# First two token groups of a projection stage: K in order of arrival, V weights loaded later, another way to sum squares, and half of a norm's scaling on ScalarE

## The reference, cut to what matters

```python
def rmsnorm(x, g):
    xf = x.astype(jnp.float32)
    y = xf * lax.rsqrt(jnp.mean(xf * xf, axis=-1, keepdims=True) + RMS_EPS)
    return (y * g.astype(jnp.float32)).astype(x.dtype)

h = rmsnorm(x, norm_g)              # (S, 2048)
z = h @ w_in                        # columns q | k | v | f | g_A | u | v_B | g_B
k = z[..., OFF_K:OFF_V]             # 8 heads x 128, an output and input of the attention
v = z[..., OFF_V:OFF_F]
logf = log_sigmoid(z[..., OFF_F:OFF_GA] + b_f)
...                                 # attention with forget bias, gated MLP over 128-chunks
y = rmsnorm(x + concat(out_a, out_b) @ w_out, final_g)
```

## Time and profile before

| | us |
|---|---|
| three timed runs, median (lowest, highest) | 1661.77 (1661.71, 1662.76) |
| the profiled execution | 1658.95 |
| its span on the slowest core, core 4 (role 0) | 1655.4 |
| spans of role 0: cores 0, 2, 4, 6 | 1654.0, 1653.5, 1655.4, 1650.1 |
| spans of role 1: cores 1, 3, 5, 7 | 1645.0, 1646.6, 1633.8, 1640.2 |
| PE busy on core 4, share of the span | 1493.5, 90% |
| ACT, DVE, POOL busy on core 4 | 589.6, 548.0, 187.8 |

### The profile page before, as it was taken

One profiled execution on the slowest core, in us unless ns is written; L12 is line 12 of the kernel. 1 busy time (PEld: TensorE's weight loads), 2 busy tenths in 40 slices (PEclk: granted clock), 3 DMA queues, 4 the chain that ended last, 5 costly groups with the idle time before them and its releaser, 6 DMA issues.

```text
span 1655.4 us, 29925 instructions; the slowest of 8 cores (1633.8 to 1655.4 us)
## 1 busy us (share of the span) xinstructions
PE 1493.5 (90%) x10986; PEld 884.7 (53%) x11164; DVE 548.0 (33%) x1035; ACT 589.6 (36%) x1011; POOL 187.8 (11%) x328
## 2 busy tenths in 40 slices
PE   2688895999699999999999999999999989999996
PEld 1567762444244444444466775776766744444443
DVE  5478710000244433333442222222222222333333
ACT  2234310111455411111115666666666681111111
POOL 2111220111233200000001101101101110000000
PEclk9899997999799999999999999999999999999999
DMA  9956399886500131222231313313212065545543
GB/s 234 231 186 228 90 163 129 130 111 92 93 1 1 24 64 42 54 42 42 58 87 26 88 28 81 78 42 82 59 46 59 26 164 166 206 152 205 201 154 118
DMA packets 90982, 168.96 MB, mean 102 GB/s; under 512 B 27728, under 2 KB 69840, under 8 KB 82000
## 3 DMA queue, kind: packets, MB, share of 16 engines
q1 hardware_dynamic: 81472, 129.17, 28.5%
q0 software_dynamic: 9360, 37.79, 13.7%
HBM read 141.68 MB, written 63.04 MB: 124 GB/s over the span
## 4 chain that ended last, share of the span: by engine, by line
PE 75%; DMA 8%; DVE 8%; ACT 5%; issue 4%; POOL 1%; SPq 0%; ACTq 0%; DVEq 0%; POOLq 0%
PE psb L291 74%; ACT arena L1026 3%; DVE arena L403 3%; DMA kT<-arena 3%; DVE arena L380 3%; DMA vo<-arena 2%; DMA arena<-bs 1%; DVE arena L901 1%; DMA arena<-xT 1%; PE psb L1097 0%; DVE arena L1099 0%; POOL arena L383 0%; POOL arena L1029 0%; ACT arena L478 0%; DVE arena L1083 0%
## 5 line engine op out<-in xcount | busy, mean ns | idle before, releaser
L291 PE MATMUL psb<-arena 128*128 128x512 bf16 (+5 forms) x10826 | 1488.0, 296 | 146.8 <-POOL arena L383 34.4
L291 PEld LDWEIGHTS psb<-arena 128*128 128x128 bf16 (+1 forms) x11004 | 876.3, 98 | 753.2 <-issue 166.0
L1026 ACT ACTIVATE arena<-psb,arena 128x512 bf16<-128x512 f32 x480 | 301.0, 634 | 167.6 <-PE psb L291 160.2
L1184 ACT ACTIVATE arena<-arena 128x2048 bf16<-128x2048 f32 x20 | 38.2, 1910 | 237.9 <-DVE arena L1179 237.9
L1179 DVE TENSOR_TENSOR arena<-psb,arena 128x512 f32<-128x512 f32 x80 | 49.7, 684 | 131.1 <-PE psb L291 131.1
L1029 POOL TENSOR_SCALAR_AFFINE_SELECT arena<-arena 128x128 bf16<-128x128 bf16 x160 | 46.8, 294 | 397.3 <-ACT arena L1026 396.7
L921 DVE SCALAR_TENSOR_TENSOR arena<-arena,psb 128x512 bf16<-128x512 f32 x40 | 27.5, 688 | 182.4 <-ACT arena L919 153.9
L403 DVE SCALAR_TENSOR_TENSOR arena<-arena 128x256 bf16<-128x256 f32 x160 | 66.0, 490 | 57.4 <-ACT arena L393 57.4
L380 DVE TENSOR_REDUCE arena<-arena 128x256 f32<-128x1024 f32 x40 | 74.6, 1928 | 12.3 <-ACT arena L378 12.3
L521 ACT ACTIVATE arena<-psb 128x512 f32<-128x512 f32 x40 | 21.7, 595 | 140.2 <-PE psb L291 92.5
L838 ACT ACTIVATE arena<-psb 128x512 f32<-128x512 f32 x40 | 23.9, 598 | 118.6 <-PE psb L291 93.3
(11 more groups left out here) (66 smaller groups left out, 391.3 us busy)
## 6 DMA issues: line engine op xcount, KB each, us to landing
arena<-xT SPq DMA_DIRECT2D x20, 1024.0 KB, 8.4
arena<-xn SPq DMA_DIRECT2D x20, 1024.0 KB, 6.9
y<-arena SPq DMA_DIRECT2D x20, 1024.0 KB, 4.8
kT<-arena SPq DMA_DIRECT2D x40, 256.0 KB, 3.0
vo<-arena SPq DMA_DIRECT2D x20, 512.0 KB, 8.1
oT_s<-arena SPq DMA_DIRECT2D x80, 128.0 KB, 2.0
arena<-oT_s SPq DMA_DIRECT2D x80, 128.0 KB, 4.9
arena<-wout POOLq DMA_DIRECT2D x16, 512.0 KB, 12.0
```

What stands on the lines that cost most here:

```text
L291: PE.op(lambda: mm(out, lhsT, rhs, start=start, stop=stop, **kw), reads=reads, writes=[PSR[bank]] if first else [], pwrites=[] if first el ...
L1026: ACT.op(lambda: act.activation(out=P[:, off:512], in_=PSB[b][:, off:512], func=AF.Exp, scale=SCALE, bias=nb[:, T, j, h:h + 1]), reads=[PS ...
L1184: ACT.op(lambda: act.activation(out=junk[q, :], in_=yb[p][q, :], func=AF.Square, accum_out=ss), reads=[yb[p].r], writes=[junk.r, R_ss[p]])
```

## The change

Five things are done, all in the first stage.

1. Squares are cut into four chunks of 64 tokens by 16 (still 1024 elements), and DVE sums 16 at a time: 64 sums of 16 an instruction instead of 256 sums of 4. The POOL add and the second matmul with ones go.
2. From pair 2 on (`ng_of`), the first 8 of the 16 columns of `norm_g` are multiplied into `xt` in place by 8 ACT copies with a per-partition scale, in `norm_a` after the squares; the mults are then 2 DVE multiplications of 128x8x128 by 1/rms and the 8 old ones for the other half.
3. K of the first two groups is emitted by pair of tokens and pair of heads as they arrive: (0;0), then (0;1), (1;0), (1;1), and so on, with a pair of tokens named first and a pair of heads behind the semicolon. The sixteen units are the same.
4. The DMAs of `wk` wait until the first pair of `xT` has landed.
5. `wf` and `wv` (on role 0 WV0, on role 1 both halves) are issued by POOL after those sixteen units instead of right behind `wk`.

```diff
-    sq = [A.alloc("sq%d" % i, [2, 4, 128], F32) for i in range(2)]
-    ssp = A.alloc("ssp", [4, 256], F32)
+    sq = [A.alloc("sq%d" % i, [KC, 64], F32) for i in range(2)]
+    ssp = A.alloc("ssp", [256], F32)
...
+    def ng_of(n):
+
+        return 0 if n < 2 else 8
...
     def norm_a(n):
         u, na, rows, w, x, rx = ninfo(n)
-        for c in range(4):
+        step = min(rows, 64)
+        for c in range(w // step):
             t = sq[c % 2]
...
+            a, n0 = c * step // rows, c * step % rows
+            ACT.op(lambda: act.activation(out=t[:, :, 0:step], in_=x[:, a, :, n0:n0 + step], func=AF.Square), reads=rx, writes=[t.r])
+            DVE.op(lambda: v.tensor_reduce(out=ssp[:, c * step:(c + 1) * step], in_=t[:, :, 0:step].rearrange("p k n -> p n k"),
+                                           axis=AX.X, op=ALU.add),
                    reads=[t.r], writes=[ssp.r] if c == 0 else [], pwrites=[] if c == 0 else [ssp.r])
-        POOL.op(lambda: g.tensor_tensor(out=ssp[:, 0:2, 0:w], in0=ssp[:, 0:2, 0:w], in1=ssp[:, 2:4, 0:w], op=ALU.add),
-                reads=[ssp.r], writes=[ssp.r])
+        for k in range(ng_of(n)):
+            ACT.op(lambda: act.activation(out=x[:, :, k, :], in_=x[:, :, k, :], func=AF.Copy, scale=gcol[:, k:k + 1]),
+                   reads=rx + [gcol.r], writes=rx if k == 0 else [], pwrites=[] if k == 0 else rx)
...
-        for c in range(2):
-            mmop(PSB[7][:, 0:w], ones[:, :], ssp[:, c, 0:w], c == 0, c == 1, [ones.r, ssp.r], 7, c == 0, c == 1)
+        mmop(PSB[7][:, 0:w], ones[:, :], ssp[:, 0:w], True, True, [ones.r, ssp.r], 7, True, True)
...
+        NG = ng_of(n)
+        for a in range(na if NG else 0):
+            DVE.op(lambda: v.tensor_tensor(out=dst[:, 0:NG, a * rows:(a + 1) * rows], in0=x[:, a, 0:NG, :],
+                                           in1=r[:, a * rows:(a + 1) * rows].unsqueeze(1).broadcast_to([128, NG, rows]), op=ALU.mult),
+                   reads=rx + [r.r], writes=[rd[a]])
+        for k in range(NG, KC):
...
-        load(POOL, WK[h][:, :, :], io["wk"][h], WK[h].r)
+        load(POOL, WK[h][:, :, :], io["wk"][h], WK[h].r, reads=xt[0].res if h == 0 else ())
...
+    for n, prs in enumerate([[(0, 0)], [(0, 1), (1, 0), (1, 1)], [(0, 2), (1, 2), (2, 0), (2, 1), (2, 2)],
+                             [(0, 3), (1, 3), (2, 3), (3, 0), (3, 1), (3, 2), (3, 3)]]):
+        norm_to(2 * n + 3)
+        for m, (p, q) in enumerate(prs):
+            if n == 3 and m == 4:
+                state["k"] = 1
+                norm_slot()
+            k_unit(p // 2, 2 * (p % 2), 2, [2 * q, 2 * q + 1])
+    load(POOL, wf[:, :, :], io["wf"], wf.r)
+    for c in range(len(WV)):
+        wv_load(c)
...
+        if kd == "K" and gi < 2:
+            continue
```

More of the change, by code:

```diff
@@ L401, in norm_b @@
             dst, rd = t[:, :, u["ii"][0] * 128:u["ii"][0] * 128 + w], [t.res[i] for i in u["ii"]]
[L402 to L405, removed]
+        NG = ng_of(n)
[4 more added lines that the diff above has]
+        for k in range(NG, KC):
+            DVE.op(lambda: v.scalar_tensor_tensor(out=dst[:, k, :].rearrange("p (a n) -> p a n", a=na), in0=x[:, :, k, :],
+                                                  scalar=gcol[:, k:k + 1], in1=r[:, 0:w].rearrange("p (a n) -> p a n", a=na),
+                                                  op0=ALU.mult, op1=ALU.mult),
                    reads=rx + [gcol.r, r.r], writes=rd if k == 0 else [], pwrites=[] if k == 0 else rd)
@@ L537, in emit @@
         POOL.op(lambda: g.memset(Vn[:, :, 128:129], 2.0), pwrites=[Vn.r])
[L538 to L541, removed]
     POOL.op(lambda: g.memset(ident[:], 1.0), writes=[ident.r])
@@ L546, in emit, with wv_load @@
     POOL.op(lambda: g.memset(m32[0:16, 16:32], 0.0), reads=[m32.r], writes=[m32.r])
+    def wv_load(c):
+        for hf in range(2):
+            load(POOL, WV[c][:, hf * 8:(hf + 1) * 8, :], io["wv"][c][:, hf * 8:(hf + 1) * 8, :], WV[c].r, part=(hf == 1))
+    for n, prs in enumerate([[(0, 0)], [(0, 1), (1, 0), (1, 1)], [(0, 2), (1, 2), (2, 0), (2, 1), (2, 2)],
[9 more added lines that the diff above has]
+        wv_load(c)
     lastK = max(i for i, (kd, gi) in enumerate(passes) if kd == "K")
@@ L578, in emit @@
                         WV.append(A.alloc("WV1", [KC, 512], BF16, hi=True))
-                        for hf in range(2):
-                            load(POOL, WV[1][:, hf * 8:(hf + 1) * 8, :], io["wv"][1][:, hf * 8:(hf + 1) * 8, :], WV[1].r, part=(hf == 1))
+                        wv_load(1)
                     k_unit(gi, i0, 2, [h, h + 1])
```

## The result

The changed kernel took 1652.37 us (median of 4 runs, 1647.87 to 1653.5), the kernel before 1662.26 on the same chip: a ratio of 0.9936, 95% interval 0.9912 to 0.9961. Forecast were 1643 and a gain of 19; it was 10. Some executions ran 4 to 15% longer at a lower granted clock on one die or both: the ratios leave these out, the medians count them.

A forecast was written before the change was run, and what follows sets the result against it. PE's waits in the first stage bound it: inputs until M4, a chain per pair to M9, then loads into V. K ending 13 earlier and V's stop 6 shorter made -19: 1661.8 to 1643, range 1630 to 1657 (8 in 10).

The forecast's parts named there:

- Step 1: DVE's reduction: 64 sums of 16 would take 1.40 us in place of 1.92, bounds 1.23 and 1.92.
- first rival: DVE's reduction costs by element, 1.92, so regrouping wins nothing there: small gain, 1655 us, chance 17%.
- Step 2: Role 0, start to pair 4's mults (M4): M4 at 92 in place of 115.25, 23 earlier, bounds 18 and 28.
- small-gain rival: Reduction stays at 1.92: M4 comes 7 later, five periods 1.04 longer each, +12 in all; 1655 us, chance 17%.
- Step 3: Role 0's period per pair from M4 on: 19.0 with the copies, one more than before, bounds 17.8 and 21.5.
- Step 4: V weights among the kT stores, role 0: WV0 costs 2.5, WV1 about 5 (0 to 10); M9 10.4 earlier.
- slower rival: V weights catch a burst's first kT store: WV0 costs 20, WV1 15, +27 in all; 1670 us, chance 7%.
- marks of 111 and 120: Fourth evacuation of the burst after M4: by 111 the forecast holds, after 120 the slower rival.
- Step 5: End of K and V, role 0: K ends 13 earlier, V's stop shrinks from 20.3 to about 14, 6 more.
- Step 6: Role 1: M4 at 100 in place of 135.82, V starts 14 to 23 earlier, "oth" groups 0; end 1624 to 1633.

The follow-up runs named there:

- e1: The changed kernel without the eight ACT copies, all 16 multiplications by norm_g on DVE: 1641.35 us, ratio 0.9917 to the kernel before.
- e9: The changed kernel, copies included, with four K buffers in place of three: 1634.89 us, ratio 0.9927 to the kernel before.
- e7: The changed kernel without the copies and with four K buffers in place of three: 1624.33 us, ratio 0.9808 to the kernel before.
- e8: The changed kernel without copies, three K buffers, WV1 asked for four K units later on role 0: 1638.18 us, ratio 0.9894 to the kernel before.
- e10: e7 with the V weights asked for right behind the K weights, the new K order kept: 1621.19 us, ratio 0.9853 to the kernel before.
- e11: e7 with wvb on role 0 asked for in 16 pieces, one behind each V unit: 1602.19 us, ratio 0.9735 to the kernel before.
- e12: e11 with the old K order and the K and V weights asked for at once: 1619.14 us, ratio 0.9788 to the kernel before.
- e2: The changed kernel without copies and regrouped sums; new order, late V weights and held-back K weights stay: 1648.91 us, ratio 0.9957 to the kernel before.

## Why the prediction was right in sign and half in size

**Step 1** failed. "If 4 elements cost 4.24 and the sum itself 2.7" has no such split: a reduction is 1.91 with 256 sums or with 64. The 57% above a plain pass were the stride, which the edit kept (512 bytes from element to element before, 256 after). I compared the row with a plain pass and took the one difference I named, the sum, without looking at the order in which the elements are read; that was the other one. The Trainium skill says so on the page Advanced Engine Details and Errata (section SBUF Cachelines): full speed needs further accesses to the same 16 bytes, and a new line each time is slower. The measurement agrees (256-byte steps 1.91, none 1.22), and the page gives no size. The rule weighed in the prediction, one element a cycle and nothing for a sum, is right once the stride is gone (1.22 against 1.226 of the plain pass), and it was the first rival.

**Step 2**: 92 forecast for M4, 100.85 measured on core 4, past the mark of 100 that was to count as wrong. M0 came at 22.9 (21.2), M2 at 57.2 (53), M3 at 81.0 (73): the reduction in each, as the small-gain rival had it, and waits for stores on the way to M3. Still 14.4 earlier than before.

**Step 3** held in its mechanism: copies 4.71 (4.8), M7 to the first evacuation 15.1 (14.5), the `kT` store next on the path, period 20.0 and 20.7 (19.0, within the bounds); the 1.04 for faster reductions did not come. The periods with five evacuations, WV0 and WV1 (21.7, 24.7, 34.2) lay outside 17.8 to 21.5, the second mark that was to count as wrong. That the copies lengthen the period was forecast, and e1 shows it: 15.8 without them. With four buffers (e9) it is 18.0 against 15.8.

**Step 4** failed in size. WV0 was to cost 2.5 and cost 4.7 (M5 to M6 24.7, the next period 20.0); WV1 was to cost 5 and cost some 14 (34.2 against 20.3). The term that failed is "a store issued 10 after it lands some 5 later": the store issued about 10 after WV1 landed only some 17 after its own issue, when both halves of WV1 were in (211.7, 218.9). The two rows that the step rested on, all stores through 21.5 after the weights, would have given its bound of 10. So the slower rival's mechanism, the first store of a burst caught, did come, at WV1 and at nearly its price there (15), but not at WV0 (20), where the burst of M4 was through in time (its fourth evacuation came at 119.0, between the marks of 111 and 120). e7 takes it away: with a buffer for every evacuation of a burst neither load costs anything.

**Step 5**: K's end was to come 13 earlier and came 16 later. `wvb` was issued 1.9 behind the last evacuation (2 forecast), but V's stop, forecast at 14, was 2.8. Both errors had one cause that step 5 missed: V's stop ends when `vo` stores get past `wvb`, and it shrinks by much of what K's end is late. So K's end, 29 later than forecast, cost core 4 only 9.5 of the 19. e8, e9 and e10 show the same from the other side (M9 moved by 9 to 14, the end of the next stage's stop on core 4 by 0 to 8). With V's stop gone the order and the late weights are worth 0.5% (e11, e12), with it 0.4% (e2), so how much of the order's own gain the stop took is not shown.

**Step 6** failed. M4 on core 5 was at 109.5 (100 forecast, 135.82 in the earlier trace rows). The first "oth" mults were still 13.6 earlier than before (280.05, 293.69), and the "oth" groups took that back: they were put at 0, bounds -8 and +10, and cost about 17 by the fourth group. e9 against e7 gives the copies 27 there. The term was priced as one ACT period of which V hides a part; what it left out is that PE stands behind the copies (5.5 at a time in e9) and that the granted clock is lower behind such a stop (0.56).

The small-gain rival (1655, the reduction by element) is close to the measured time, but not by its own sum: it had neither WV1's 14 nor role 1's lost gain, and V's stop hid most of the rest. That the time fell into 1630 to 1657 was in part luck: K's end was 29 late and the reduction gained nothing, and the stops of 20.3 and 16.4 gave back 17 and 7 where 6 were forecast.

## What to carry to other kernels

Before you credit a microsecond won early, look for the next stop on a load or store: it can give back what is late and take what is early. Here a fourth buffer won 34 at M9 and 1.1% at the end, and spreading the load that made the stop 0.7% more. Price work put on an engine by what queues behind it there, on every role and in every stage that runs the same code, and PE's clock behind the stop with it. When you take work off an engine, look at what it held back: without POOL's add WV1 went ahead of the burst and took back what the regrouping had won.

## What the runs showed of the hardware

- A step between f32 elements costs on both engines, for 1024 elements a partition: DVE's reduction 1.91 reading at 256 bytes against 1.22, ACT's square 1.95 writing at 64 bytes against 1.06.
- Beside a casting load of 2 x 1 MB a `kT` store of 256 KB took 15 to 19 to land (2.1 alone in the earlier trace rows), 17.0 when it was issued 10 us after the load; one issued in the same moment as the load took 4.4. The stores landed just behind the second half of the load: 223.4 and then 224.2 before, 218.9 and then 220.5 in the changed kernel.
- PE's stops cost twice: on role 1 in e9 the granted clock was 0.56 and 0.53 in stretches of 4 us behind two stops of 5.5 and 5.4, with 16 matmuls in each, and 1.00 in the next 4 us, with 28 and 29.
